# Feed-forward output by one level of Strassen's recursion, in a two-layer decoder trunk on one Trainium2 core

## The reference

```python
def conv_gated_ffn(h, w_in, conv_w, conv_b, w_out):
    a = h @ w_in
    gate, up = a[..., :FFN_DIM], a[..., FFN_DIM:]            # FFN_DIM = 2816
    ...
    return (jax.nn.silu(conv) * up) @ w_out                  # (512 x 2816) @ (2816 x 1024)
```

## Time and profile before

| | |
|---|---|
| median of 3 runs | 1498.79 us (1498.66 to 1498.87) |
| the profiled execution's own time | 1498.81 us |
| its span in the profile | 1496.9 us |
| TensorE busy | 1483.0 us (99%) |
| VectorE busy | 847.7 us (57%) |
| GpSimd busy | 796.9 us (53%) |
| ScalarE busy | 675.6 us (45%) |
| granted clock of TensorE, mean | 0.998 |
| HBM traffic | 142.14 MB, mean 95 GB/s |

### The profile page before, as it was taken

How to read it: one execution, slowest core, us unless ns; L and a number is a source line. 1 busy time by engine, 2 the same in 40 slices (tenths; PEclk the granted TensorE clock), 3 DMA queues, 4 the chain that set the end, 5 groups by cost and what they waited for, 6 DMA issues and landing times.

```text
span 1496.9 us, 19989 instructions
## 1 busy us (share of the span) xinstructions
PE 1483.0 (99%) x6808; PEld 1235.4 (83%) x6808; DVE 847.7 (57%) x1294; ACT 675.6 (45%) x1019; POOL 796.9 (53%) x980
## 2 busy tenths in 40 slices
PE   9999999999999999999999999999999999999997
PEld 6888888888888888888888888888888888888886
DVE  7999997455555411169875655646655555511145
ACT  6887886433333322246573543635633333322243
POOL 5343344666666755457345253551666666755453
PEclk9999999999999999999999999999999999999999
DMA  4121111323222322243132322321232222332221
GB/s 179 57 71 55 43 56 59 111 99 98 98 98 98 126 99 97 86 163 105 56 141 99 109 90 90 134 99 43 85 113 91 96 92 98 120 111 97 93 79 63
DMA packets 42838, 142.14 MB, mean 95 GB/s; under 512 B 4256, under 2 KB 10528, under 8 KB 42784
## 3 DMA queue, kind: packets, MB, share of 16 engines
q1 hardware_dynamic: 41248, 138.82, 27.2%
q10 hardware_dynamic: 1536, 2.61, 0.5%
HBM read 139.32 MB, written 2.10 MB: 94 GB/s over the span
## 4 chain that ended last, share of the span: by engine, by line
PE 96%; DVE 2%; ACT 1%; DMA 1%; issue 0%; POOL 0%; SPq 0%; POOLq 0%; DVEq 0%; ACTq 0%
PE bank L606 27%; PE bank L610 26%; PE bank L609 26%; PE bank L884 3%; PE bank L889 3%; PE bank L888 3%; PE bank L684 2%; PE bank L664 1%; PE bank L665 1%; PE bank L695 1%; PE bank L694 1%; DMA x<-in_xT 1%; PE bank L1037 0%; DVE sumsq L1126 0%; PE bank L667 0%
## 5 line engine op out<-in xcount | busy, mean ns | idle before, releaser
L552 POOL TENSOR_TENSOR wl<-raw,wh 128x256 fp32r<-128x256 f32 x752 | 617.4, 853 | 471.1 <-ACT wh L1712 471.1
L606 PE MATMUL bank<-xh,wh 128*128 128x512 f32 (+1 forms) x1160 | 451.6, 389 | 1.2 <-POOL wl L552 0.8
L610 PE MATMUL bank<-xh,wl 128*128 128x512 f32 (+1 forms) x1160 | 450.2, 388 | 0.0
L609 PE MATMUL bank<-xl,wh 128*128 128x512 f32 (+1 forms) x1160 | 449.9, 388 | 0.0
L1712 ACT ACTIVATE wh<-raw 128x1024 fp32r<-128x1024 f32 (+1 forms) x212 | 234.9, 1108 | 475.3 <-PE bank L606 387.6
L606 PEld LDWEIGHTS bank<-xh,wh 128*128 128x128 f32 x1160 | 217.9, 188 | 46.8 <-DVE xl L1132 1.7
L610 PEld LDWEIGHTS bank<-xh,wl 128*128 128x128 f32 x1160 | 217.9, 188 | 44.9
L609 PEld LDWEIGHTS bank<-xl,wh 128*128 128x128 f32 x1160 | 218.0, 188 | 43.8
L568 POOL TENSOR_TENSOR wl<-raw,wh 128x256 fp32r<-128x256 f32 x160 | 127.3, 826 | 190.6 <-ACT wh L1712 190.6
L1152 DVE TENSOR_TENSOR x<-x,bank 128x512 f32<-128x512 f32 x56 | 38.5, 687 | 251.1 <-PE bank L610 251.1
L610 PE MATMUL bank<-yh,wl 128*128 128x512 f32 x352 | 137.0, 389 | 0.0
(11 more groups left out here) (224 smaller groups left out, 2325.2 us busy)
## 6 DMA issues: line engine op xcount, KB each, us to landing
raw<-in_w SPq DMA_DIRECT2D x180, 512.0 KB, 3.2
raw<-in_w SPq DMA_DIRECT2D x32, 704.0 KB, 4.0
rc<-in_w SPq DMA_DIRECT2D x16, 512.0 KB, 4.1
w_end<-in_w SPq DMA_DIRECT2D x8, 512.0 KB, 4.2
rb<-in_w SPq DMA_DIRECT2D x8, 512.0 KB, 6.1
x<-in_xT SPq DMA_DIRECT2D x4, 512.0 KB, 7.2
pin<-in_pT ACTq DMA_DIRECT2D x2, 512.0 KB, 3.2
rotary<-in_consts ACTq DMA_DIRECT2D x1, 512.0 KB, 3.5
```

The source lines that it names most:

```text
L552: last = nc.gpsimd.tensor_tensor(wl[:, slot, cols], part[:, cols], wh[:, slot, cols].bitcast(F32), ALU.subtract)
L606: first = mm(out, ah_, bh_, start=start, stop=False, skip_group_check=True)
L609: mm(out, ah_, bl_, start=False, stop=False, skip_group_check=True)
L610: return mm(out, al_, bh_, start=False, stop=stop, skip_group_check=True)
```

## The change

The feed-forward output, 1024 x 2816 weights by 2816 x 512 activations, is cut into halves each way: the weights by output chunk (first index: 1 for output chunks 4 to 7, 2 for output chunks 0 to 3) and by hidden chunk (second index: 1 for even f, 2 for odd f), y by hidden chunk (first index) and by tokens (second index: `early` for 0 to 255, `late` for 256 to 511). The eight half-size products become seven (Winograd's form): their left operands are A11, S1 = A21 + A22, S3 = A11 + A21, S2 = S3 + A22, A22, S4 = S2 + A12 up to signs, and A12, each of four pieces of 11 blocks, so 28 pieces of 33 products of 128 x 256 a layer. The right operands are Y11, T1 = Y11 - Y12, T3, Y12, T4, Y22, Y21, each 11 x 256 columns, split into high and low as before.

- **Weight sums.** GpSimd issues 16 transfers a layer that add a 704 KB tile from HBM onto one already in SBUF (`accum_op=ALU.add`, in the order of `SUMMED`). SP issues 18 plain loads of 704 KB a layer (`LOADS`) in place of 16. S1 uses the two regions of raw (r0, r1); S3, S2 and S4 grow one on the other in four buffers s0 to s3, two of which overlie space that the input stage still uses.
- **Weight lows.** GpSimd makes none in this stage. VectorE makes wl of each piece with one instruction of 1408 columns (`low_part`). It makes two before its loop, and then the low of piece j + 2 after it has taken the result of piece j - 1.
- **Results.** Each piece's bank (256 columns) is added to or taken from x by VectorE (`take`), for A11 to both halves at once, for S2 in two instructions.
- **Right operands.** In the input stage VectorE gets five instructions of 256 columns for each pair of chunks (T1, two lows, T2, T3) in place of two lows of 512. In the output stage ScalarE makes five copies of 11 x 256 = 2816 columns (`right_highs`), VectorE five lows of 2816 columns and T4 (`right_lows`, `t4`), at places fixed in `beside`.
- **Norm and p.** The x parts, squares and the split of p are at fixed places in the same tables.

The diff, cut to its core:

```diff
-DMA_SCRATCH = 256
+DMA_SCRATCH = 512
...
+PIECES = ([("A11", m) for m in range(K2)]
+          + [(kind, m) for m in range(K2) for kind in ("S1", "S3")]
+          + [("S2", 0), ("S2", 1), ("A22", 0), ("S2", 2), ("A22", 1), ("S2", 3), ("A22", 2), ("A22", 3)]
+          + [("S4", 0), ("S4", 1), ("S4", 2), ("A12", 0), ("S4", 3), ("A12", 1), ("A12", 2), ("A12", 3)])
...
+LOADS = [("A11", 0, "s0"), ("A11", 1, "r0"), ("A11", 2, "r1"), ("A22", 0, "r0"), ("A22", 1, "r1"),
+         ("A11", 3, "s3"), ("A11", 1, "s1"), ("A11", 2, "s2"), ("A22", 2, "r0"), ("A22", 3, "r1"),
+         ("A22 alone", 2, "r2"), ("A22 alone", 3, "r3"), ("A22 alone", 0, "r0"), ("A22 alone", 1, "r1"),
+         ("A12", 0, "r0"), ("A12", 1, "r1"), ("A12", 2, "r2"), ("A12", 3, "r3")]
...
+SUMMED = [("S1", 0), ("S3", 0), ("S1", 1), ("S3", 1), ("S1", 2), ("S3", 2), ("S1", 3), ("S3", 3),
+          ("S2", 0), ("S2", 1), ("S2", 2), ("S2", 3), ("S4", 0), ("S4", 1), ("S4", 2), ("S4", 3)]
+ADDED = {"S1": "A21", "S3": "A21", "S2": "A22", "S4": "A12"}
...
 # SP
+                for what, m, into in LOADS:
+                    if (what, m) == ("A11", 0):
+                        sp_eng.wait_ge(w_low, end - 2)
+                    elif what == "A11" and into[0] == "r":
+                        sp_eng.wait_ge(w_low, end - 2 + m)
+                    elif into == "s3":
+                        sp_eng.wait_ge(f_begun, f_count(layer, 0))
+                    elif into[0] == "s":
+                        sp_eng.wait_ge(y_full, FC * (layer + 1))
+                    elif what == "A22" and m < 2:
+                        piece_low("A11", m + 1)
+                    elif what == "A22":
+                        piece_low("S1", m - 2)
...
 # GpSimd
+                for kind, m in SUMMED:
+                    into = ("r0", "r1")[m % 2] if kind == "S1" else f"s{m}"
+                    if kind == "S1":
+                        pool.wait_ge(*filled(layer, "A22", m, into))
+                    elif kind == "S3" and m in (1, 2):
+                        pool.wait_ge(*filled(layer, "A11", m, into))
+                    else:
+                        before = {"S3": "A11", "S2": "S3", "S4": "S2"}[kind]
+                        pool.wait_ge(f_low, f_count(layer, PIECE[before, m]))
+                    f_sem, _ = filled(layer, kind, m, into)
+                    nc.gpsimd.dma_start(ROW[into], out_weights(FFN_OUT_TILES * layer, ADDED[kind], m),
+                                        accum_op=ALU.add).then_inc(f_sem, 16)
...
 # TensorE
+                for q, (kind, m) in enumerate(PIECES):
+                    out = bank[m if kind in ("S1", "S4") else K2 + m][:, 0:HALF]
+                    pe.wait_ge(f_low, f_count(layer, q))
...
+                    for k in range(FH):
...
+                        last = three(out, *blk(piece_slot(layer, q), k), high[:, k, :], low_[:, k, :], opens and k == 0,
+                                     k == FH - 1, begins=k == 0, begun=f_begun)
...
 # VectorE, input stage
-                        vec.tensor_tensor(yf[:], cv, up[:], ALU.mult).then_inc(y_full, 1)
-                        dve.wait_ge(y_high, at + 1)
-                        low(one(yl, f), yf[:], one(yh, f), y_low)
+                        vec.tensor_tensor(one(y, f), cv, up[:], ALU.mult).then_inc(y_full, 1)
...
+                            vec.tensor_tensor(one(y, f - 1)[:, late], one(y, f)[:, late], one(y, f - 1)[:, late], ALU.add)\
+                                .then_inc(t2_full, 1)
+                            dve.wait_ge(t2_full, FH * layer + i + 1)
+                            vec.tensor_tensor(one(y, f - 1)[:, early], one(y, f - 1)[:, late], one(y, f - 1)[:, early],
+                                              ALU.subtract).then_inc(t3_full, 1)
...
 # VectorE, output stage
+                beside = {
+                    1: lambda: right_lows(1, zl, Y11, zh, 1),
+                    6: lambda: (right_lows(2, xa_l, Y12, xa_h, -1), t4()),
+                    12: lambda: right_lows(3, ya_l, Y12, ya_h, -1),
...
+                    28: lambda: (x_lows(6), squares(6)),
+                }
+                for q in range(2):
+                    low_part(q)
+                for j in range(N_PIECES + 1):
+                    if j:
+                        take(j - 1)
+                    if j + 2 < N_PIECES:
+                        low_part(j + 2)
+                    if j in beside:
+                        beside[j]()
...
 # ScalarE, output stage
+                right_highs(1, zh, Y11, 1.0)
+                piece_high(layer, RING - 1)
+                for j in range(1, N_PIECES - RING + 1):
+                    if j in (18, 20):
+                        beside[j]()
+                    piece_high(layer, j + RING - 1)
+                    if j in beside and j not in (18, 20):
+                        beside[j]()
```

More of the change, by code:

```diff
@@ L58 @@
 FFN_IN_TILES, FFN_OUT_TILES = 2 * FC, 2 * KC
+K2 = KC // 2
 PL_TILES = KC * PC // W8 + KC
@@ L507, in ret_loads, with out_loads, piece_low @@
                     out(RH - 1, t)
+            def out_loads(layer, at11):
+                def piece_low(*piece):
+                    sp_eng.wait_ge(f_low, f_count(layer, PIECE[piece]))
+                end = N_PL[layer] - (OTHERS_LOW if layer else 0)
+                for what, m, into in LOADS:
[11 more added lines that the diff above has]
+                        piece_low("S1", m - 2)
+                    elif what == "A22 alone" and m >= 2:
+                        sp_eng.wait_ge(right_low, 5 * layer + 1)
+                    elif what == "A22 alone":
+                        piece_low("S1", m + 2)
+                    else:
+                        piece_low("A22", m)
+                    f_sem, _ = filled(layer, what, m, into)
+                    sp_eng.dma_start(REGION[into], blocked(out_weights(at11, what, m))).then_inc(f_sem, 16)
+                for m in range(2):
+                    piece_low("A12", m)
             at8, at11, n0 = ATT_TILES, 0, ATT_TILES
@@ L1118, in norm_open, with add_square @@
                 vec.memset(sumsq[:], 0.0).then_inc(sumsq_zero, 1)
-            def add_square(norm, k, par_):
+            def add_square(norm, k, par_, square=None):
                 at = KC * norm + k
+                part = SQUARE[par_][:] if square is None else square
                 dve.wait_ge(sumsq_zero, norm + 1)
@@ L1178, in x_phase_before_embed @@
                 take_proj(layer, 0)
-                x_low_part(norm, last)
+                x_lows(last)
                 take_proj(layer, 1)
-                add_square(norm, last, last % 2)
+                squares(last)
                 take_proj(layer, 2)
@@ L1357, in ffn @@
                                                      ALU.add).then_inc(conv_step, 1)
+                        if u:
+                            dve.wait_ge(t1_high, FH * layer + i + 1)
+                            low(one(ya_l, i), one(y, f - 1)[:, late], one(ya_h, i), t1_low)
                         dve.wait_ge(chunk_done, c + 2)
@@ L1729, in tile_high, with piece_high @@
                 copy(wh[:, slot, 0:blocks * P], raw_slot(ring, r, blocks), w_high)
+            def piece_high(layer, q):
+                kind, m = PIECES[q]
+                if q < RING - 1:
+                    act.wait_ge(w_begun, N_PL[layer] - RING + q + 2)
+                else:
+                    act.wait_ge(f_begun, f_count(layer, q - RING + 1))
+                what = "A22 alone" if kind == "A22" else kind
+                act.wait_ge(*filled(layer, what, m, piece_home(q)))
+                copy(blocked(wh[:, piece_slot(layer, q), :]), piece_source(q), f_high)
             def square_free(norm, k):
@@ L1895, in turn @@
-                        act.wait_ge(y_full, at + 1)
-                        copy(one(yh, f), yf[:], y_high)
+                        ahead(2 * u + 1)
+                        if u == 0:
+                            act.wait_ge(y_full, at + 1)
+                            copy(one(xa_h, i), one(y, f)[:, early], y11_high)
                 with act.Fori(0, last) as i:
-                    turn(i, n0, RING)
-                turn(last, n0 + RING * last, 0)
-                act.wait_ge(y_low, FC * (layer + 1))
```

297 lines of the change are left out of this document (225 added, 72 removed), and 3 rows, old and new, of the table LOADED.

## The result

The changed kernel takes **1573.27 us** (median of 4 runs, 1569.63 to 1574.3) beside 1498.74 us for the one before: ratio 1.0493, interval 1.0475 to 1.0511. I had given 1509 and a range up to 1550. It is slower, as forecast, but by 74.5 us and not by 10.

The account below looks back on a forecast made before the run. TensorE, busy 99% of the span, was taken to bound the kernel; -8.8 + 4.5 + 2.2 + 1.4 + 0.5 + 5.2 = +5.0 us a layer, +10.0 on 1498.8, gave 1509 us, range 1490 to 1550.

Parts of the forecast that it names:

- the price of a sum: Output stage: a sum moves 3.0 us, between bounds of 1.8 (plain load) and 3.6 to 3.8 (two loads).
- six pieces of room from piece 12 on: Output stage: from piece 12 on, sums have six pieces or more of room, so no later stalls.
- the signs of being wrong: TensorE never waits behind piece 0, S pieces wait for DMA one after another, or 256-column products run at another pace.
- slower still: Rival: sums go through GpSimd one behind another, moving 6 us each; +38 us a layer, 1575 us; chance 0.10.
- Products: Output stage: 924 products of 256 columns at 0.120 us replace 528 of 512, gaining 8.8 us a layer.
- Start of the stage: Output stage: TensorE idles 4.5 us a layer until VectorE has made piece 0's weight low.
- Clock: Low clock behind the 4.5 us start wait: bounds nothing and 4 us a layer, taken as nothing.
- A11's last piece and piece 4: Output stage: late load delays piece 3 by 2.2 us; VectorE's work behind its low delays piece 4 by 1.4 us.
- VectorE's burst at place 6: Output stage: two instructions of 2816 columns, 6.2 us, beside a take and a low make piece 9 late by 5.2 us.
- The draw: Rival: sums at the price of plain loads; +1 us a layer, 1501 us; chance 0.13.
- Input stage and embedding: Input stage's five instructions of 0.42 us, and the embedding with 48 products of cover: both cost nothing.
- The end of the forecast's range: Upper end 1550 us, taking in the double price of sums with clock losses and part of the slow case.

Follow-up runs that it names:

- ring2048: Changed kernel with 2048 instead of 512 bytes a partition for GpSimd's descriptors, three attention constants moved to make room: 1542.83 us.
- nosums_warm: Changed kernel without its sums, plus 18 unread products of 512 columns in TensorE's wait at the start of each output stage: 1497.50 us.
- plain: Changed kernel with GpSimd's 16 transfers a layer replacing the tile instead of adding to it, waits and HBM bytes kept: 1508.39 us.
- nosums: Changed kernel with no sums issued by GpSimd, each S piece using the tile that lies in its place: 1496.80 us.

## Why the prediction was wrong

**The step that failed** is the price of a sum: "I take 3.0 us of moving", with the next one following at once. A sum takes 4.5 us of moving by itself, and since one alone is under way a step is 6.9 us. With that, 16 sums are 110 us of a stage of 120, and TensorE waits for nearly every piece up to 13; I had counted six pieces of room from piece 12 on, and pieces 12 and 13 wait 2.65 and 2.66 us. The room came with piece 14. Of the signs of being wrong that the prediction names, one came: pieces of S wait for transfers one after another. The forecast that came nearest is "slower still" (one behind another, 1575 us), to which I gave 0.10 with no row for or against it. It had the mechanism, one behind another, though not its cause, and its price of 6 us was 0.9 short. That 1575 lies within 2 us of the result is partly luck: its +38 a layer stands there without a working from the 96 us of sums.

What could have led there: the diff doubles `DMA_SCRATCH`, so the space for descriptors is something that this kernel has to count, and I went past that line. The trace of before could not give the price, since no transfer in it adds and GpSimd issues none. My upper end was the wrong one: two loads are the price of a sum among others (3.7 us, ring2048), not of one alone.

Point by point:
- **Products:** held. 0.120 us apart over hundreds, -8.8 us a layer. The lower price for an isolated product did not appear.
- **Start of the stage:** held. 4.27 us against 4.5, released by VectorE's low of 1408 columns, which took 1.62 against 1.6.
- **Clock:** I took nothing, with bounds of 0 and 4 us a layer. Behind the first wait it is 1.5 us (16 products about 0.21 apart in place of 0.12). Over the whole stage it is some 11 (12.9 less the tails), as TensorE stops before one piece in two and the clock falls again. Most of that probably cost nothing more, since in the same time TensorE would have waited for the sums; that is argued, no run shows it. The waits are a consequence of the failed step. My reason for taking nothing ("pieces 3 and 4 are late by their weights anyway") is what nosums_warm bears out. The Trainium skill describes this pattern ("TensorE: Matmul & The Clock Gate", section on HAM oscillation): waits for a transfer between short stretches of work bring the clock down again and again. The windows at 0.90 and 0.87 agree; the waits in them are 0.4 to 4.9 us long.
- **A11's last piece and piece 4:** 2.2 and 1.4 us forecast, 0.43 and 2.30 measured. Without sums they are 0.16 and 0.92.
- **VectorE's burst at place 6:** its length held (6.2 us), its cost depends on whether piece 8 is early. 5.2 us were forecast for sums of 3.0 us, and 1.5 to 1.9 for sums at the plain price. In plain, at that price, piece 9 waits 4.69 us in layer 0 and 2.24 in layer 1, so there the term was too small: piece 8 was itself just late (0.51 us) and not ahead. In the changed kernel piece 9 waits 2.35 us; its copy ended at 576.2, its low began only behind the burst, at 578.13, so some 1.9 us of that are the burst's. In nosums, where the pieces are ahead, it costs nothing. VectorE's timeline of plain, and TensorE's piece 9:

```profile
557.98 3.09 DVE L1332 SCALAR_TENSOR_TENSOR xa_l<-y,xa_h 128x2816 fp32r<-128x2816 f32 x1 [0.82 <-ACT xa_h L1945]
561.11 3.09 DVE L1337 TENSOR_TENSOR y<-y 128x2816 f32<-128x2816 f32 x1
...
564.45 1.62 DVE L1260 TENSOR_TENSOR wl<-s,wh 128x1408 fp32r<-128x1408 f32 x1
```
```profile
566.12 0.58 PE L743 MATMUL psum<-zh,wh 128*128 128x256 f32 x1 [4.69 <-DVE wl L1260]
```

- **The draw** (sums at the price of plain loads, 1501 us) is what plain measures: 1508.4. It is 7 above: in layer 0 by the burst and a clock of 0.69 behind it (566 to 575 us).
- **Input stage and embedding:** the time held; all of the 70.9 us is in the output stages. The price didn't: the five added instructions take 0.70 to 0.91 us on average and not 0.42, which cost nothing because VectorE waits for TensorE there.
- **The end of the forecast's range** took in half of the slow case, and the result lies 23 us above it. The part of the slow case that I left out was the likeliest part of it.

## What to carry over

A recursion of Strassen's kind saves an eighth of the columns, here 15.0 us a layer on paper. The finer grain of the products takes 6.2 of that and the start of the pipeline of weights 4.3, so that 4.5 are left to pay for 16 sums. Measure an operation that the old trace doesn't have by itself before a schedule is built on it, alone and queued, since the two prices can differ by two (6.9 and 3.7 us here). When a change raises a resource's size by a constant, ask how many operations in flight that size allows.

## What was not expected of the hardware

- A 704 KB transfer that adds takes 4.5 us of moving alone and a step of 6.9 us; queued with others 3.7 us, where plain ones need 1.8.
- With 512 bytes of each partition for GpSimd's descriptors one such transfer is under way at a time, with 1024 three, with 2048 as many as were issued here, up to six; of plain ones three are under way with 512.
- While adding transfers are queued, a load in pieces of half a kilobyte from another queue gets almost nothing: 0.40 MB in 20 us, in as many packets (774) as the adding ones have (777), each a tenth as large.
- The granted clock fell behind waits of 2.4 us (0.59) and 4.3 us (0.52), and also over a stretch in which each wait was 0.4 to 2.5 us (0.90 from 525 to 560 us).
